# Expert stage of a decoder layer: the fourth and fifth product of each step change places

## The chip, the cores and the metric

One core of a Trainium2 chip runs the whole layer as one program. The metric is the device time of the program in microseconds, the median of several runs. TensorE is called PE here, VectorE DVE, ScalarE ACT, GpSimd POOL, and SyncE SP; SP issues the loads of the weights. All engines run on their own and meet in semaphores.

## What is computed

A decoder layer on 512 tokens of width 1024: attention and a state-space branch, merged and projected back, then a mixture of 32 experts of which each token takes four. Only the expert stage matters here. The reference gathers the rows of each expert and does, for each of them:

```python
gu = xb @ w1[e] + b1[e]                      # 1024 -> 2048
gate, up = gu[:, :D_EXPERT], gu[:, D_EXPERT:]
gate = jnp.minimum(gate, SWIGLU_LIMIT)
up = jnp.clip(up, -SWIGLU_LIMIT, SWIGLU_LIMIT)
act = (up + 1.0) * (gate * jax.nn.sigmoid(SWIGLU_ALPHA * gate))
yb = act @ w2[e] + b2[e]                     # 1024 -> 1024
return yb * wts[:, None].astype(yb.dtype)
```

All weights are float32: w1 of one expert is 8 MiB, w2 is 4 MiB, so the 32 experts have 384 MiB.

## The kernel before

The expert stage is the last block of the kernel. The experts are ranked by the number of their rows and taken in pairs, one from the 16 with most rows ("big", room for 112 rows) and one from the rest ("small", room for 64). Weights come in units of 1 MiB, twelve for an expert: eight of w1 (`(1, n)`, 128 rows of 8 KB) and four of w2 (`(2, n)`, 256 rows of 4 KB).

A big expert's unit is split before it is used: ACT copies the raw unit to a rounded high part (`split_at`, line 1970), DVE makes the low part as raw less high (line 2087), and PE multiplies three times, high by high, low by high and high by low (line 1854 for w1, 1866 for w2). The raw slot is free once DVE is done. A small expert's unit is multiplied in float32 as it is (line 1874 for w1, 1883 for w2), two column groups of PE side by side; its slot is free when PE is done.

The stage runs in steps of twelve units, an S step and a B step in turn, 15 pairs of steps in a loop and a last S step behind it. An S step does w1 of the small expert and w2 of the big one before it; a B step does w1 of the next big expert and w2 of the small one. Which unit stands at which of a step's twelve positions is written out by hand in `STEP` (line 45): an entry `(1, n)` is a unit of the expert whose w1 is due, `(2, n)` one of the expert whose w2 is due. So in an S step the entries `(1, n)` are small and the entries `(2, n)` big, in a B step the reverse. `PLACE` (line 47) turns a position into the running number of that expert's kind.

Four engines walk through the same list:

- SP (`step`, line 1744) issues the load of each position into one of six raw slots in turn (`RAW`, `slot_of`). It first waits in `freed` for the unit six positions earlier: for DVE's low part if that was a big expert's unit, for PE's product if it was a small one's. Loads are issued at line 1728.
- ACT and DVE (`step_s`, `step_b`) take the big expert's units of the step in order, into three split buffers (`SPLIT`). ACT's high part waits for the load, and for PE to have used the unit three before.
- PE (`unit`, `step_s`, `step_b`) takes all twelve. Ahead of the first entry `(2, n)` (`FIRST2`) it writes the bias of the second product into its bank: `bias2_b` in an S step (line 1840), `bias2_s` in a B step (line 1846). Behind the last `(1, n)` (`LAST1`) it transposes the next rows.

POOL gathers the rows of the next experts by indirect DMA, and makes the tiles that pick an expert's bias (`pick_big`, `pick_small`), each after a wait for a count of units used. Results go out by DMAs that ACT issues (lines 2017 and 2026). ACT has the evacuations of the banks in the same list as its splits, at places that don't depend on `STEP` beyond their being ahead of or behind its units.

Of the kernel before, what the change touches and what calls it, by code (L numbers as in the profile page):

```python
# [41 lines left out]
NB = E + NOV + 1  # L42
YROWS = NBIG * CAP + NSM * CS
FILL = NOV * CAP // 7
STEP = ((1, 0), (1, 1), (1, 2), (2, 0), (1, 3), (1, 4), (1, 5), (2, 1), (1, 6), (1, 7), (2, 2), (2, 3))
FIRST2, LAST1 = STEP.index((2, 0)), STEP.index((1, 7))
PLACE = {"S": [("S", n) if m == 1 else ("B", n) for m, n in STEP],
         "B": [("B", 4 + n) if m == 1 else ("S", KT + n) for m, n in STEP]}
RAW, SPLIT = 6, 3
# [112 lines left out]
def decoder_layer(nc, x, small, consts, onehot_rows, gffn, rel_bias, par, w_mix, w_dt, w_tail, w_rt, w1, w2, b12,  # L162
                  tok_ids, pads, out):
    with ExitStack() as ctx:
# [1513 lines left out]
        with nc.Block() as block:  # L1678
# [37 lines left out]
            def _(sp):  # L1716
# [13 lines left out]
                def freed(j, kind, p):  # L1730

                    q = p + (12 if kind == "B" else 0) - RAW
                    if q < 0 and isinstance(j, int) and j == 0:
                        sp.wait_ge(lo_ready, KT + q + 1)
                        return
                    if q < 0:
                        j, q = j - 1, q + 24
                    of, i = PLACE["S" if q < 12 else "B"][q % 12]
                    if of == "B":
                        sp.wait_ge(lo_ready, b_unit(j, i) + 1)  # L1740
                    else:
                        sp.wait_ge(s_used, s_unit(j, i) + 1)

                def step(j, kind, e1, e2):
                    for p, (m, n) in enumerate(STEP):
                        freed(j, kind, p)
                        load(slot_of(kind, p), m, n, e1 if m == 1 else e2)
# [33 lines left out]
            def _(pe):  # L1781
# [106 lines left out]
                def unit(j, kind, p):  # L1888

                    m, n = STEP[p]  # L1890
                    of, i = PLACE[kind][p]
# [72 lines left out]
            def _(act):  # L1964
# [7 lines left out]
                def split(j, kind, p):  # L1972

                    of, i = PLACE[kind][p]
                    assert of == "B"
                    split_at(b_unit(j, i), (KT + i) % SPLIT, slot_of(kind, p), landed(j, kind, p))
# [52 lines left out]
                def step_s(j, more):  # L2029
# [3 lines left out]
                    for p in range(12):  # L2033
                        if STEP[p][0] == 2:
                            split(j, "S", p)
# [333 lines left out]
```

## Time and profile before

| | us |
|---|---|
| three runs | 2086.09, 2095.89, 2097.14 |
| median | 2095.89 |
| profiled execution, its span | 2092.0 |
| expert stage in it, about | 980 to 2052 |

The page gives the span of the profiled execution from its first to its last instruction; a time with what lies around the span isn't shown for it. In the page's 40 slices a slice is 52.3 us, and a digit is the busy share in tenths. PE is busy 90% of the span, DVE 52%, ACT 45%, POOL 13%. The mean granted clock of TensorE is 0.955 of 2.4 GHz. "Releaser" is what ended an engine's idle time; a load's time to landing runs from its issue by SP to its last byte, and so holds the time that it queues behind other loads.

### The profile page before, as it was taken

How to read it: one execution, taken by the hardware profiler on the slowest of the kernel's cores; microseconds unless marked ns; L12 is line 12 of the kernel's file. 1: busy time of each engine (PE TensorE's matmuls, PEld its weight loads, DVE VectorE, ACT ScalarE, POOL GpSimd, SP SyncE). 2: the span in 40 equal slices, each digit the busy share in tenths (PEclk: the TensorE clock that was granted, in tenths of full speed). 3: DMA queues.
4: the chain of work that ended last, by engine and by line, in shares of the span. 5: the costliest groups of instructions: out<-in, count | busy, mean ns of one | idle time of the engine just before them, and what ended most of it. 6: DMA issues, size and time to landing. Idle time of an engine off the chain costs nothing.

```text
span 2092.0 us, 27150 instructions
## 1 busy us (share of the span) xinstructions
PE 1875.1 (90%) x8654; PEld 1313.1 (63%) x8654; DVE 1097.2 (52%) x1343; ACT 949.8 (45%) x1350; POOL 276.5 (13%) x327
## 2 busy tenths in 40 slices
PE   7999999999989999871999999999999998999991
PEld 5887887788767888661656555565555655565550
DVE  6557756855755333325545544554435544455443
ACT  5566666666655222311535443454434443354430
POOL 0312222231220000004000000011001110011002
PEclk9999999999999999975999999999999999999996
DMA  5023122212203222431899999999999999999996
GB/s 200 31 88 118 40 96 100 90 54 91 88 10 101 100 90 100 153 157 52 336 404 397 408 394 403 393 407 397 398 406 395 409 394 405 398 396 404 407 397 227
DMA packets 110267, 519.66 MB, mean 248 GB/s; under 512 B 14912, under 2 KB 18024, under 8 KB 77240
## 3 DMA queue, kind: packets, MB, share of 16 engines
q1 hardware_dynamic: 99480, 487.76, 60.0%
q0 software_dynamic: 6144, 19.94, 3.1%
q10 hardware_dynamic: 4608, 11.54, 1.4%
q8 instruction: 17, 0.28, 0.1%
q14 instruction: 18, 0.15, 0.0%
HBM read 502.98 MB, written 26.49 MB: 253 GB/s over the span
## 4 chain that ended last, share of the span: by engine, by line
DMA 20%; PE 19%; DVE 6%; ACT 4%; issue 3%; POOL 1%; ACTq 0%; SPq 0%; POOLq 0%; DVEq 0%
DMA big<-in_w 19%; PE bank L1854 9%; DVE w_lo L2087 5%; PE bank L1866 4%; PE bank L1874 4%; ACT w_hi L1970 3%; PE bank L1883 2%; POOL big L2261 1%; DVE x_lo L2099 1%; DMA big<-y_all,last_idx 0%; DVE keep L2124 0%; ACT keep L1997 0%; DVE keep L2184 0%; PE bank L1809 0%; PE bank L1790 0%
## 5 line engine op out<-in xcount | busy, mean ns | idle before, releaser
L2087 DVE TENSOR_TENSOR w_lo<-big,w_hi 128x2048 fp32r<-128x2048 f32 x192 | 439.0, 2294 | 417.7 <-ACT w_hi L1970 417.4
L1970 ACT ACTIVATE w_hi<-big 128x2048 fp32r<-128x2048 f32 x192 | 366.3, 1916 | 431.4 <-DMA big<-in_w 405.5
L1874 PE MATMUL bank<-big,keep 128*64 128x512 f32 x1024 | 230.9, 598 | 0.0
L1117 PE MATMUL bank<-h_hi,wm_hi 128*128 128x512 f32 x384 | 157.2, 409 | 4.1 <-DVE wend L898 2.9
L1874 PEld LDWEIGHTS bank<-big,keep 128*64 128x64 f32 x1024 | 69.3, 137 | 137.8 <-issue 137.8
L1854 PE MATMUL bank<-w_hi,x_hi 128*128 128x512 f32 x512 | 146.9, 409 | 8.9 <-DVE w_lo L2087 8.5
L1117 PE MATMUL bank<-h_hi,wm_lo 128*128 128x512 f32 x384 | 151.0, 393 | 0.0
L1117 PE MATMUL bank<-h_lo,wm_hi 128*128 128x512 f32 x384 | 150.3, 391 | 0.0
L1866 PE MATMUL bank<-w_hi,a_hi 128*128 128x512 f32 x256 | 91.4, 440 | 59.2 <-DVE w_lo L2087 58.9
L1854 PE MATMUL bank<-w_lo,x_hi 128*128 128x512 f32 x512 | 138.6, 393 | 0.0
L1854 PE MATMUL bank<-w_hi,x_lo 128*128 128x512 f32 x512 | 137.9, 391 | 0.0
L1854 PEld LDWEIGHTS bank<-w_hi,x_hi 128*128 128x128 f32 x512 | 91.2, 189 | 64.4 <-DVE w_lo L2087 43.1
L1883 PE MATMUL bank<-big,keep 128*64 128x512 f32 x512 | 120.0, 602 | 0.0
L1499 DVE TENSOR_TENSOR g_lo<-keep,g_hi 128x1024 fp32r<-128x1024 f32 x39 | 47.8, 1225 | 125.2 <-ACT g_hi L1424 122.8
L1854 PEld LDWEIGHTS bank<-w_lo,x_hi 128*128 128x128 f32 x512 | 96.7, 189 | 21.6
L1854 PEld LDWEIGHTS bank<-w_hi,x_lo 128*128 128x128 f32 x512 | 96.7, 189 | 20.9
L1866 PEld LDWEIGHTS bank<-w_hi,a_hi 128*128 128x128 f32 x256 | 48.1, 204 | 89.8 <-DVE w_lo L2087 81.9
L837 DVE SCALAR_TENSOR_TENSOR big<-bank,par_sb,big 128x511 f32<-128x511 f32 (+2 forms) x96 | 71.7, 747 | 31.7 <-ACT big L588 23.2
L1117 PEld LDWEIGHTS bank<-h_hi,wm_hi 128*128 128x128 f32 x384 | 72.5, 189 | 24.5 <-issue 5.8
L1144 PE MATMUL bank<-vz_hi,h_hi 128*128 128x384 f32 x256 | 87.2, 341 | 0.0
L1866 PE MATMUL bank<-w_lo,a_hi 128*128 128x512 f32 x256 | 85.9, 419 | 0.0
L1144 PE MATMUL bank<-vz_hi,h_lo 128*128 128x384 f32 x256 | 85.9, 336 | 0.0
(314 smaller groups left out, 3306.9 us busy)
## 6 DMA issues: line engine op xcount, KB each, us to landing
big<-in_w SPq DMA_DIRECT2D x384, 1024.0 KB, 10.5
big<-in_w_mix SPq DMA_DIRECT2D x72, 512.0 KB, 3.3
keep<-in_w_tail SPq DMA_DIRECT2D x47, 512.0 KB, 3.2
y_all<-in_x SPq DMA_DIRECT2D x7, 1280.0 KB, 7.9
y_all<-keep ACTq DMA_DIRECT2D x16, 448.0 KB, 8.1
y_all<-keep ACTq DMA_DIRECT2D x32, 128.0 KB, 7.1
keep<-in_x SPq DMA_DIRECT2D x4, 512.0 KB, 4.9
big<-in_x SPq DMA_DIRECT2D x4, 512.0 KB, 4.5
```

The costliest lines, as they stand in the source:

```text
L837: ins = dve.scalar_tensor_tensor(out=conv[:, n, s:T], in0=proj_b[n % 2][:, 0:T - s], scalar=w, in1=conv[:, n, s:T], op0=ALU.mult, op1=ALU.add)
L1117: ins = pe.matmul(proj_b[n % 2][:], w[:, k], h[:, k], start=(k == 0 and w is hi and h is h_hi), stop=(k == KT - 1 and w is lo))
L1144: ins = pe.matmul(proj_b[t % 2][:, 0:VZ], h[:, k, t * P:(t + 1) * P], w[:, k], start=(k == 0 and h is h_hi and w is hi), stop=(k == KT - 1 ...
L1499: dve.tensor_tensor(lo, graw[:, m % GRAW], hi.bitcast(F32), ALU.subtract).then_inc(glo_ready.sem, 1)
L1854: ins = pe.matmul(bank[c][:], x_part, w_part[:, s, c * 512:(c + 1) * 512], start=False, stop=n == KT - 1 and w_part is w_hi and x_part is lo)
L1866: ins = pe.matmul(bank[4 + c][:], a_part, w_part[:, s, o:o + 512], start=False, stop=k == KT - 1 and w_part is w_hi and a_part is lo)
L1874: ins = pe.matmul(bank[2 * (c // 2)][r, :], x_s[:, n], raw[:, s, c * 512:(c + 1) * 512], start=False, stop=n == KT - 1)
L1883: ins = pe.matmul(bank[4][CS * c:CS * (c + 1), :], a_s[:, k % 4, CS * (k // 4):CS * (k // 4 + 1)], raw[:, s, o:o + 512], start=False, stop ...
L1970: act.activation(w_hi[:, s], raw[:, r], ACT.Copy).then_inc(hi_ready, 1)
L2087: dve.tensor_tensor(w_lo[:, s], raw[:, r], w_hi[:, s].bitcast(F32), ALU.subtract).then_inc(lo_ready, 1)
L2099: dve.tensor_tensor(lo[:, k, 0:CAP], turned(half), hi[:, k, 0:CAP].bitcast(F32), ALU.subtract).then_inc(done.sem, 1)
L2261: pool.indirect_dma_start(fin[:, n], None, y_all, bass.IndirectOffsetOnAxis(ap=last_idx[:, n:n + 1], axis=0)).then_inc(fin_in[n // TOPK], 16)
```

## The change

In `STEP` the entries `(2, 0)` and `(1, 3)` at positions 3 and 4 (counted from 0) change places. `FIRST2` is computed from the list and goes from 3 to 4; `LAST1` stays 9. Everything that walks through `STEP` or `PLACE` follows: loads and their slots, splits, products. In an S step the four products at the start are then small, small, small, small, and the big expert's first w2 unit is fifth; in a B step four big ones stand at the start, and the small expert's first w2 unit is fifth. No instruction is added or removed.

```diff
-STEP = ((1, 0), (1, 1), (1, 2), (2, 0), (1, 3), (1, 4), (1, 5), (2, 1), (1, 6), (1, 7), (2, 2), (2, 3))
+STEP = ((1, 0), (1, 1), (1, 2), (1, 3), (2, 0), (1, 4), (1, 5), (2, 1), (1, 6), (1, 7), (2, 2), (2, 3))
 FIRST2, LAST1 = STEP.index((2, 0)), STEP.index((1, 7))
 PLACE = {"S": [("S", n) if m == 1 else ("B", n) for m, n in STEP],
          "B": [("B", 4 + n) if m == 1 else ("S", KT + n) for m, n in STEP]}
```

## Rows read from the trace of the kernel before

**Rows 1.** The page: span, and busy tenths of PE and DMA by slice.

```profile
span 2092.0 us, 27150 instructions
...
PE   7999999999989999871999999999999998999991
...
DMA  5023122212203222431899999999999999999996
```

**Rows 2.** Windows of two pairs of steps, with the columns.

```profile
core 0: us, PE busy (x) PEld busy (x) DVE busy (x) ACT busy (x) POOL busy (x), PEclk, DMA share, GB/s
1203.60:1270.30 66.70, 61.76 (x283) 36.96 (x282) 33.42 (x22) 28.74 (x24) 5.50 (x8) 1.00 1.02 399
...
1403.70:1470.20 66.50, 62.45 (x279) 37.43 (x278) 33.33 (x22) 28.73 (x24) 7.75 (x8) 0.97 1.02 401
```

**Rows 3.** DMA view, 1203.6 to 1270.3: rate in 40 slices, packets, loads' queue.

```profile
GB/s 432 423 423 398 381 236 243 383 410 426 434 393 423 440 408 418 398 413 420 430 437 393 432 398 425 322 302 283 420 437 440 386 427 435 403 423 400 415 408 437
DMA packets 4975, 26.60 MB, mean 399 GB/s; under 512 B 464, under 2 KB 464, under 8 KB 2928
...
q1 hardware_dynamic: 4479, 25.16, 95.2%
```

**Rows 4.** Loads (line 1728) to landing: 1060 to 1980; the one at 1018.8.

```profile
DMA to landing us min/median/max: 5.8/10.6/14.0
...
DMA to landing us min/median/max: 4.8/4.8/4.8
```

**Rows 5.** Chain of waits, last S step: start, duration, what.

```profile
2013.39 9.32 DMA big<-in_w
...
2024.68 2.30 DVE w_lo L2087
...
2035.24 5.69 PE bank L1866 x24
```

**Rows 6.** Timeline, S step: start, duration, engine, line; idle before in brackets.

```profile
1416.34 1.91 ACT L1970 ACTIVATE w_hi<-big 128x2048 fp32r<-128x2048 f32 x1 [3.87 <-DMA big<-in_w]
...
1417.07 0.50 PE L1840 MATMUL bank<-bias_hl,pick_b 64*128 64x512 f32 x2
1418.28 2.29 DVE L2087 TENSOR_TENSOR w_lo<-big,w_hi 128x2048 fp32r<-128x2048 f32 x1 [5.54 <-ACT w_hi L1970]
...
1420.63 1.22 PE L1866 MATMUL bank<-w_hi,a_hi 128*128 128x512 f32 x2 [3.06 <-DVE w_lo L2087]
...
1431.03 0.74 PE L1866 MATMUL bank<-w_hi,a_hi 128*128 128x512 f32 x2 [0.62 <-DVE w_lo L2087]
```

**Rows 7.** Window of the w2 unit at position 3, columns as in rows 2.

```profile
1420.60:1425.00 4.40, 4.37 (x12) 3.28 (x12) 0.00 (x0) 0.00 (x0) 0.00 (x0) 0.64 1.01 414
```

**Rows 8.** Loads: S position 4; S 9 to 11; B position 3, issued 1437.8.

```profile
L1728 SPq DMA_DIRECT2D big<-in_w x1: 333/333/333, 1408.9 to 1408.9; - x1
...
DMA to landing us min/median/max: 9.9/9.9/9.9
...
L1728 SPq DMA_DIRECT2D big<-in_w x3: 333/384/384, 1420.7 to 1428.9; - x3
...
DMA to landing us min/median/max: 7.0/7.8/10.9
...
DMA to landing us min/median/max: 10.0/10.0/10.0
```

**Rows 9.** Timeline, start of the B step.

```profile
1448.90 2.29 DVE L2087 TENSOR_TENSOR w_lo<-big,w_hi 128x2048 fp32r<-128x2048 f32 x1 [1.07 <-ACT w_hi L1970]
...
1451.70 1.92 ACT L1970 ACTIVATE w_hi<-big 128x2048 fp32r<-128x2048 f32 x1 [2.83 <-DMA big<-in_w]
...
1454.08 0.39 PE L1846 MATMUL bank<-bias_hl,pick_s 128*128 128x512 f32 x1
1454.39 1.94 PE L1883 MATMUL bank<-big,keep 128*64 128x512 f32 x8
...
1457.05 2.29 DVE L2087 TENSOR_TENSOR w_lo<-big,w_hi 128x2048 fp32r<-128x2048 f32 x1 [1.11 <-ACT w_hi L1970]
```

## The prediction

> **What bounds the kernel now.** Read the page first: the last 19 of its 40 slices, the expert stage, show PE and DMA both at 9 tenths or more [rows 1]. The change lives there only, so the question is which of the two sets its pace. The windows over pairs of experts answer it: of four pairs in a row the first takes 66.7 us and the last 66.5, the DMA share is 1.02 in both, 399 and 401 GB/s are moved, and PE is busy for 61.8 and 62.5 us [rows 2]. PE has some 4 us to spare in each pair; the DMA engines have none. The DMA view of one pair says what fills them: of 26.60 MB the 24 weight loads of 1 MiB are 25.16, and gathered rows and results written out the other 1.44 [rows 3]. Where neither crosses, the slices of that view lie around 420 GB/s, so a load needs 1.049 MB / 420 GB/s = 2.5 us; 24 of them are 60 us, and the other 6.6 us are what 1.44 MB in short pieces cost.
>
> Being busy isn't enough: a queue that runs dry now and then would show as well. So look at how far ahead the loads are issued. From 1060 to 1980 us a load lands 5.8 to 14.0 us after its issue, median 10.6 [rows 4]. A load that found the queue empty (1018.8 us, after the gap at the start of the stage) landed in 4.8 us [rows 4]. The smallest distance of 920 us, 5.8, is 1.0 us above that, so before every load another one was still under way. The queue never runs dry. That SP waits between its loads, with six slots taken, is then the sign of a full queue and not of a late release.
>
> The chain of waits names ACT, DVE and PE behind a load, since it runs from the load through the split to the product and back to the slot [rows 5]. That a slot's release stands on it doesn't make the release late: the load that it permits has 7 us and more of other loads ahead of it.
>
> **The change, part by part.** In an S step the first unit of the big expert's w2 (call it B0; w2 of the big expert, split into a high and a low part) goes from position 3 to 4, and the small expert's w1 unit n=3 (S3) from 4 to 3. In a B step the same swap puts the big expert's w1 unit 3 ahead of the small expert's first w2 unit. Instructions, bytes, slots and split buffers are the same in number: 0 us of work are added or removed. The order is read by SP (loads), ACT and DVE (splits) and PE (products), so all four move together; POOL's list doesn't move, but two of its waits count units (lines 2223 and 2229, the tiles that pick the bias) and end one unit, up to 3 us, later. Both tiles are next read by a bias product at the start of a later step, with seven units between, so at 2.5 us and more a unit they still come over 14 us early; without that cover PE would wait those 3 us.
>
> *S step, by the pair at 1404 us.* PE waits 3.06 us for B0's low part [rows 6]: the load of position 3 landed at 1416.3, where ACT's idle ends; ACT's high part took 1.91, DVE's low part 2.29, PE began at 1420.63. Its three S units had ended by 1417.07, the bias product by 1417.57. An S unit takes PE 1.8: the three between B0's end at 1425.0 [rows 7] and the idle before B1 take 1431.03 - 0.62 - 1425.0 = 5.4 us. After the change the load of position 3 holds S3, needs no split, and PE multiplies it at once: 1417.1 + 1.8 = 1418.9; bias 0.5, to 1419.4. B0 is now the load of position 4, which lands at 1408.9 + 9.9 = 1418.8 [rows 8]; through ACT and DVE (1.91 + 2.29 and some 0.08 between) it is ready at 1423.1. So the wait before B0 does not go: it is 1423.1 - 1419.4 = 3.7 us, 0.6 longer, as the load moves back by one place (2.5 us) and one S unit takes only 1.8. B0 then takes 4.4 us as before [rows 7] (to 1427.5), S4 and S5 take 3.6 (to 1431.1). B1 is a position that doesn't move: PE began it at 1431.03, after 0.62 us of idle that DVE's low part ended. After: 1431.1. The longer wait before B0 is taken from the idle before B1, and behind B1 nothing is changed. Sum for PE: 0.1 us late at most, and the queue has 7 us in hand for that.
>
> *Its slots.* Six slots in turn, so position 9 waits for position 3, 10 for 4, 11 for 5, and the next step's 0 for 6. Position 9: before when B0's low part was made (issue 1420.7), after when S3 is used (1418.9). Position 10: before when S3 was used (1425.0 + 1.8, so issued at 1427, to landing 7.0 us, the shortest of this pair), after when B0 is split (1423.1): 4 us earlier. Position 11: before 1428.9 with 7.8 us to landing, after S4's use at 1429.3: 0.5 us later, 7.3 [rows 8]. So the shortest distance goes from 7.0 to 7.3, against 4.8 for a queue just empty. The margin is a little wider, and a wider margin on a full queue is worth 0 us.
>
> *B step.* PE does w1 units 0 to 2, then from 1454.08 the bias (0.4 us), the S unit, and unit 3 behind it [rows 9]. After, unit 3 is the load of position 3, which landed at 1437.8 + 10.0 = 1447.8 [rows 8]; DVE is free of unit 2 at 1448.90 + 2.29 = 1451.2, so unit 3's low part is ready at about 1453.5, and PE begins it without idle at 1454.0, where the bias stood. A B unit takes 2.85 (5.69 for two [rows 5]): to 1456.8; bias 0.4 and S unit 1.8 to 1459.0, with the S unit's load (position 4) landed when ACT's idle ends, at 1451.7 [rows 9]. Unit 4's low part is ready at 1457.05 + 2.29 = 1459.34 in both orders, and PE can't begin unit 4 before. Again 0. Position 10 is now freed by the S unit, at 1459.0, position 9 by a split, at 1453.5; position 10's load would be issued some 2 us later than now, with those of positions 8 and 9 still queued in front of it. 0 us.
>
> *Start and end.* The stage's only dry spot is at its start: the load at 1018.8 waits for the first S unit's use. Positions 0 to 2 are untouched, so it stays where it is; position 9 would wait for one S unit more, about 1 us, with two loads ahead of it. 0 us. The end hangs on B1 of the last S step (load issued at 2013.39, landed 9.32 later, DVE's part at 2024.68), then on two S units, B2, B3, the results and four S units [rows 5]; all stand at unmoved positions. 0 us.
>
> *What no row shows.* Which load is under way while results and gathered rows cross the engines. In the S step these 0.52 MB (64 rows of 4 KB gathered, as much written) press the rate to 236 and 243 GB/s for two slices of 1.67 us, in the B step 0.92 MB (112 rows each way) press it to 322, 302, 283 for three [rows 3]. Against 420 that is 2 x 1.67 x 180/420 = 1.4 us and 3 x 1.67 x 118/420 = 1.4 us. In the S step w1 rows of 8 KB take the place of w2 rows of 4 KB in that spot. Bounds: a gain of the whole 1.4 us a pair, or nothing; as a loss, the same 1.4 once more. The value taken is 0, since in the B step positions 4 and 5 are w1 loads already and the dip is there all the same.
>
> The Trainium skill speaks to this ("DMA: Bandwidth & Descriptors", Queues, rings and completion order): each DMA engine takes turns between its queues, a whole packet at a time. By that rule larger pieces in the load's queue would win it a larger share while a write is pending and only delay the write, for which nobody waits; the engines' total stays and the sum stays 0. No row here separates share from total.
>
> **The rivals.** *Faster:* the S step's dip goes, as the load that meets the writes has larger pieces. For it: per byte the S dip costs nearly twice the B dip. Against it: the B dip stands with w1 loads. At the full price 15 pairs x 1.4 = 21 us, 2075; if it only falls to the B step's cost per byte, 0.6 x 15 = 9 us, 2087.
>
> *Slower:* TensorE's clock. After the waits before B0 the granted clock is low: it is 0.64 of 2.4 GHz from 1420.6 to 1425.0, that is mostly the 1.2 GHz level, and B0's 12 products take 4.4 us [rows 7] where B units run at 2.85 [rows 5]. The pair at 1203 us had 1.00 in the mean and PE busy 61.8, those after 0.97 [rows 2], so not each wait brings it. A wait of 3.7 us could bring it each time and keep it through S4 and S5: 3.6 us more for the two, and for B0 0.6 to 1.5 more where it now runs at full clock in part or whole. PE's 62.5 would become 66.1 to 67.6 in a pair of 66.5: PE would take over as the bound with up to 1.1 us a pair, 16 us over 15 pairs: 2112. It decides where PE's busy time of a pair passes 66.5. Against it: once PE is late, it waits less before B0, and the clock stays up.
>
> The Trainium skill warns of the same ("TensorE: Matmul & The Clock Gate", Part 1: The HAM clock gate): the slow clock is the default and activity releases it. That the low level follows the idle wait here agrees with it; by that page alone a longer wait would speak for this rival, at the price above.
>
> *It doesn't do what it says:* the swap would fill PE's wait before B0 with S3 if the loads stayed where they are, 1.8 us of 3.06. They move with it, and PE isn't the bound: even with them left in place no time would be won.
>
> **How the numbers follow.** The profiled span is 2092.0 us; the runs' median is 2095.9, 0.2% above, and the runs reach from 2086.1 to 2097.1. Change 0 + 0 + 0 = 0: 2092.0 for a profiled execution, 2095.9 for the median. Forecast (DMA remains the bound, nothing shifts): 0.76, by itself 2087 to 2103. Faster rival: 0.12. Slower rival: 0.12. The range for 8 in 10 takes in the nearer part of both: 2080 to 2106. A measurement of this kernel can tell some 0.5% (10 us) from no change; beyond that: faster 0.12, within 0.76, slower 0.12.
>
> **What would show it.** In the profile after: pairs of 66.5 us and a DMA share of 1.02; the wait before B0 still there, at 3.3 to 4.0 us; idle before B1 gone; the shortest time from issue to landing above 5 us; PE's busy time of a pair below 64. The forecast is wrong if a pair takes 65.1 (the dip gone) or over 67.5 with PE busy throughout, or if loads land in under 5 us.

## The result, and the profile after

The changed kernel took 2084.23 us in the median (2080.85 to 2086.80), the kernel before 2094.97 beside it: a ratio of 0.995, interval 0.9926 to 0.9974. Timed again beside each other, with more runs, the same two kernels stood at 2085.00 and 2090.82, ratio 0.997, interval 0.9955 to 0.9986. The change is a small gain of 0.3 to 0.5%, some 6 to 11 us. The forecast was no change (2095.9). Its range of 2080 to 2106 held the time, but only because it took in part of a rival; that there would be no change was wrong.

The page of the kernel after, where it answers to [rows 1]:

```profile
span 2080.8 us, 27121 instructions
...
PE   7999999999988999870999999999999999999991
...
DMA  6023122212202322531899999999999999999995
```

Nothing moved there: PE and DMA are both full through the expert stage. Of the 11.2 us between the spans 2.1 lie ahead of the stage (its seventh load is issued at 988.7 before and 986.5 after), which the change doesn't touch. The rest lies in the pairs. Two pairs after, columns as in [rows 2]:

```profile
1202.00:1267.60 65.60, 61.91 (x273) 36.86 (x272) 33.23 (x22) 28.88 (x24) 6.71 (x8) 0.95 1.01 398
...
1398.90:1465.30 66.40, 62.52 (x276) 37.63 (x275) 33.24 (x22) 28.89 (x24) 6.57 (x8) 0.95 1.01 399
```

The engines' work is the same, the DMA share is full, and still a pair is done sooner: the DMA engines need less time for the same bytes. The landings of the loads tell where. From the issue and the time to landing of each load (as in [rows 4, 8]) the interval between any two landings follows; the means over 14 pairs, in us:

| stretch | before | after |
|---|---|---|
| S step, positions 3 to 6 (four loads) | 12.85 | 12.50 |
| B step, positions 3 to 6 | 13.22 | 12.88 |
| the other 16 loads of the pair | 40.24 | 40.28 |
| pair | 66.3 | 65.7 |

One profile a kernel is thin evidence for such a table: a second profile of the unchanged kernel, taken later, has 12.38, 13.12, 40.23 and 65.7 us in these four rows. So the pair's 0.6 us isn't told from scatter, and neither is the S row; only the B row, checked over more profiles below, holds.

Four loads alone on the engines take 4 x 2.49 = 10.0 us. In both stretches something else crosses: a gather of token rows, and then the results. The DMA view of 1060 to 1980 us has the time to landing of both gathers, first before, then after (`s_idx` is the small expert's gather, `g_idx` the big one's; the last number is the median from issue to landing):

```profile
keep<-h_rows,s_idx POOLq DMA_INDIRECT x14, 8.2
keep<-h_rows,g_idx POOLq DMA_INDIRECT x13, 9.5
```

```profile
keep<-h_rows,s_idx POOLq DMA_INDIRECT x14, 7.7
keep<-h_rows,g_idx POOLq DMA_INDIRECT x13, 8.0
```

The big gather landed 1.5 us sooner. The rate in 40 slices of 0.6 us, about one big gather, before (1436 to 1460 us) and after (1431 to 1455):

```profile
GB/s 430 396 410 423 423 423 423 423 423 423 369 416 416 410 423 430 437 287 294 294 314 328 321 355 314 451 444 403 437 451 437 423 369 396 410 430 430 416 430 423
```

```profile
GB/s 300 410 396 423 423 423 410 423 423 437 423 437 423 437 437 423 403 266 314 294 294 348 348 444 451 355 478 410 416 410 451 437 437 416 376 403 403 444 451 389
```

The dip is as deep as before (266 to 348 GB/s against 287 to 355) but six slices long in place of eight (with a single slice of 355 two slices behind). While the gather is on, the engines move some 300 GB/s, not 420; what makes its crossing shorter saves time for the whole stream. So the question for the experiments was: what shortens it?

The trace also counts the packets (one for each row that is moved). Here is the DMA view of one big gather from its first row to its last, 1511.5 to 1516.1 before, then 1507.1 to 1510.3 after; q0 is the gathers' queue:

```profile
DMA packets 274, 1.50 MB, mean 325 GB/s; under 512 B 30, under 2 KB 30, under 8 KB 153
...
q0 software_dynamic: 126, 0.46, 31.3%
```

```profile
DMA packets 275, 1.04 MB, mean 326 GB/s; under 512 B 23, under 2 KB 23, under 8 KB 272
...
q0 software_dynamic: 127, 0.46, 44.8%
```

The packets under 2 KB carry next to nothing. In both views 112 of those between 2 and 8 KB are the gathered rows. What is left are the loads' rows: 121 of 8 KB and 11 of 4 KB before, 3 of 8 KB and 137 of 4 KB after. So beside each gathered row about one row of the loads passes, be it long or short, at the same total rate; with short ones the same gather is through in 3.1 us and not in 4.4. The loads' rows that pass are those of position 4 (w1 before, w2 after), though position 3 lands only 2.6 us after the gather's first row (1514.2 against 1511.6) in this pair before: a load's rows cross well ahead of its landing.

The results have no part in the dip. Their rows (q10) cross behind it, in the B step of the pair at 1203 us before from 1250.3 to 1255:

```profile
DMA packets 340, 2.02 MB, mean 431 GB/s; under 512 B 37, under 2 KB 37, under 8 KB 149
...
q10 hardware_dynamic: 128, 0.46, 23.9%
```

The other steps of the forecast, in the timeline of the pair at 1399 us:

```profile
1418.34 1.22 PE L1866 MATMUL bank<-w_hi,a_hi 128*128 128x512 f32 x2 [3.70 <-DVE w_lo L2087]
...
1423.76 3.73 PE L1874 MATMUL bank<-big,keep 128*64 128x512 f32 x16
...
1427.42 0.73 PE L1866 MATMUL bank<-w_hi,a_hi 128*128 128x512 f32 x2
```

PE waits 3.70 us before B0, and no longer before B1, as forecast; B0 takes 5.4 us (1418.34 to 1423.76), 1 us more than before. PE's busy time of a pair hardly moved: 62.5 and 61.9 us in the windows above, 62.5 and 61.8 before [rows 2].

### The profile page after: what moved, and what is told of

It reads as the page before. It is cut to its first block, busy times and chain, and to the rows that moved or that the text cites. A ratio compares the mean times of both kernels' runs of the same rounds, so it can differ in the third digit from the quotient of the medians.

```text
span 2080.8 us, 27121 instructions
## 1 busy us (share of the span) xinstructions
PE 1873.9 (90%) x8654; PEld 1315.7 (63%) x8654; DVE 1095.8 (53%) x1343; ACT 949.4 (46%) x1350; POOL 279.3 (13%) x327
## 4 chain that ended last, share of the span: by engine, by line
PE 27%; DMA 15%; DVE 5%; ACT 3%; issue 2%; POOL 1%; ACTq 0%; SPq 0%; POOLq 0%; DVEq 0%
DMA big<-in_w 14%; PE bank L1854 14%; PE bank L1866 5%; PE bank L1883 4%; DVE w_lo L2087 4%; PE bank L1874 3%; ACT w_hi L1970 3%; POOL big L2261 1%; PE bank L1797 0%; DMA big<-y_all,last_idx 0%; DVE x_lo L2099 0%; DVE keep L2184 0%; DVE keep L2124 0%; PE bank L1790 0%; ACT keep L2014 0%
## 5 line engine op out<-in xcount | busy, mean ns | idle before, releaser
L1866 PE MATMUL bank<-w_hi,a_lo 128*128 128x512 f32 x256 | 87.3, 425 | 0.0
```

The costliest lines, as they stand in the source:

```text
L1866: ins = pe.matmul(bank[4 + c][:], a_part, w_part[:, s, o:o + 512], start=False, stop=k == KT - 1 and w_part is w_hi and a_part is lo)
```

## The experiments

Each was timed beside the kernel before on its chip, and the ratio is to that kernel. How finely a ratio can be read, the unchanged kernel tells: timed in the same way against itself it stood at 1.0011 (0.9997 to 1.0024). "B stretch" is the time of the four loads at B positions 3 to 6, "S stretch" the same in the S step, both as above.

### Loads or products

First theory (A): the DMA engines are the bound, and a gather costs less against w1's rows of 8 KB, which now stand at position 3, than against w2's of 4 KB. Rival (B): PE's new order frees a slot earlier. The load order and the product order can be changed apart:

```diff
+PROD = <the other order>
-FIRST2, LAST1 = STEP.index((2, 0)), STEP.index((1, 7))
+FIRST2, LAST1 = PROD.index((2, 0)), PROD.index((1, 7))
...
-                    m, n = STEP[p]
+                    m, n = PROD[p]
+                    p = STEP.index((m, n))
```

> Loads in the new order, products in the old one (slots, splits and waits follow the loads). Theory A (the DMA engines stay the bound, and a gather of token rows costs them less while loads with rows of 8 KB are in the queue than with rows of 4 KB): the whole gain of the change, ratio to the kernel before 0.994 to 0.997; a gathered row set lands as fast as in the changed kernel. Rival B (the gain comes from PE's order: it frees a slot earlier): no gain, 0.999 to 1.002. Rival C (nothing but scatter between runs): 1.000.

Measured: 2122.03 us, ratio 1.0152 (1.0131 to 1.0173).

> Loads in the old order, products in the new one. Theory A: no gain, 0.999 to 1.002, gathers as slow as in the kernel before. Rival B: 0.994 to 0.997. Rival C: 1.000.

Measured: 2106.36 us, ratio 1.0077 (1.0059 to 1.0094).

Both were slower, which neither theory had. From 1060 to 1980 us the loads' time to landing was, in the first and in the second:

```profile
DMA to landing us min/median/max: 4.7/10.6/14.1
...
DMA to landing us min/median/max: 4.7/9.7/14.3
```

4.7 us is the time of a load that finds nothing, or as good as nothing, ahead of it [rows 4]. With the loads new and the products old, S position 9 waits for the slot of the w1 unit that is loaded first but multiplied only behind B0: in the pair at 1404 us it is issued at 1439.54, after the load before it had landed (1438.96), and the landing behind it comes 5.3 us later in place of 2.5. The other way round it is B position 9 (issued 1465.28, the load before it lands at 1466.58). Once a pair the queue ran dry, and a pair took 68.3 and 67.0 us (before 66.3): this is what it costs when the loads aren't issued far enough ahead. The runs don't tell A from B by time. But the B stretch fell to 12.93 us with the new load order and was 13.27 with the old: the gain goes with the order of the loads. The time to landing says the opposite, 10.4 us for the big gather with the new load order (9.4 with the old). In the packets its rows cross in 3.6 us (4.2 with the old order), but the first of them 6.1 us after the gather's issue, where it is 4.1 to 4.2 us in all other runs; why it starts late there isn't shown. So it is the crossing that counts, and the time to landing stands for it only where the start is the same.

### The length of the rows

> The kernel before with w2 laid out so that its loads have rows of 8 KB as those of w1; order, bytes and waits unchanged. Theory A: gathers get as short as in the changed kernel or shorter, which is worth 0.6 us a pair or 10 us, and the 8 w2 loads of a pair take 2.49 in place of 2.55 us, worth 0.5 us a pair or 7 us: together some 2078, ratio 0.990 to 0.994. Rivals B and C: only the second part, 0.996 to 0.998.

```diff
-                        src = w2[bass.ds(e, 1), 2 * n:2 * n + 2].rearrange("a k p n -> p (a k) n")
-                        dst = raw[:, s].rearrange("p (k n) -> p k n", k=2)
+                        src = w2[bass.ds(e, 1), n].rearrange("a p n -> (a p) n")
+                        dst = raw[:, s]
...
-    w2 = np.asarray(i["w2"][0]).reshape(E, 8, P, D)
+    w2 = np.asarray(i["w2"][0]).reshape(E, 4, 2, P, D).transpose(0, 1, 3, 2, 4).reshape(E, 4, P, 2 * D)
```

Measured: 2087.00 us, ratio 0.9974 (0.9962 to 0.9986), as rivals B and C had it. The gathers landed in 8.2 and 9.3 us, as before: only the second part came, that w2's loads get as fast as w1's (2.49 in place of 2.55 us). Theory A falls: rows of 8 KB at position 3 don't make a gather cheap.

> The changed kernel with the same w2 layout. Theory A: the order no longer matters, so the same time as the kernel before with that layout (within 0.2%), ratio 0.990 to 0.994. Rival B: the two gains add, 0.4 to 0.5% below the kernel before with that layout.

Measured: 2083.36 us, ratio 0.9959 (0.9943 to 0.9975). The big gather took 9.3 us here too. This is the changed kernel's order, and its gain at the big gather is gone: it hung on w2 having rows of 4 KB. The time is above the expected 0.990 to 0.994, since no gather got cheaper, and not told from the run before it. So a new theory (D): a gather is cheap where *short* rows are queued, and the change put them right: position 4, not 3.

> The changed kernel with w1 laid out so that all its loads have rows of 4 KB like those of w2. Theory D (a gather shares the engines with the loads for a shorter time where the loads in the queue have short rows; the changed kernel has a w2 load at position 4, right where the big gather runs, and that is why its big gather lands in 8.0 in place of 9.5 us): both gathers land as fast or faster than in the changed kernel (big 8.0 us or less, small 7.5 or less). The 16 w1 loads of a pair take 2.55 in place of 2.49 us, 1.0 us a pair, so 0.998 to 1.003 of the kernel before. Rival E (row length has no part in it, only the instant at which a gather is issued): gathers as in the changed kernel or in the one before (9.5 us), 1.002 to 1.007.

```diff
-    w1 = np.asarray(i["w1"][0]).reshape(E, KT, P, 2 * D)
+    w1 = np.asarray(i["w1"][0]).reshape(E, KT, P, 2, D).transpose(0, 1, 3, 2, 4)
```

(and the load as w2's.) Measured: 2094.98 us, ratio 1.0018 (1.0005 to 1.0032); gathers 7.4 and 7.8 us, loads 2.56 us each. As theory D has it, on both counts. By itself the run doesn't exclude rival E, which allowed the changed kernel's gathers and a time from 1.002 on.

### One step at a time, and the change once more

> The swap in S steps alone. Theory D with the small gather's part: the four loads at S positions 3 to 6 take 12.5 in place of 12.85 us, B steps as in the kernel before (13.2): half of the gain, ratio 0.997 to 0.999. If the two steps are coupled by the queue, the queue runs dry in places as it did with loads and products in different orders: slower than the kernel before.

Measured: 2088.68 us, ratio 0.9991 (0.9978 to 1.0004).

> The swap in B steps alone. Theory D: the four loads at B positions 3 to 6 take 12.9 in place of 13.2 us and the big gather lands in about 8.0 us, S steps as before: the other half, ratio 0.997 to 0.999. If the steps are coupled: slower than the kernel before.

Measured: 2087.87 us, ratio 0.9977 (0.9963 to 0.9992).

The edit of both is one table for each kind of step in place of `STEP`:

```diff
+ORD = {"S": <one order>, "B": <the other>}
...
-                    for p, (m, n) in enumerate(STEP):
+                    for p, (m, n) in enumerate(ORD[kind]):
...
-                    m, n = STEP[p]
+                    m, n = ORD[kind][p]
```

The big gather in the traces, first with the swap in S steps, then in B steps:

```profile
keep<-h_rows,g_idx POOLq DMA_INDIRECT x13, 9.4
```

```profile
keep<-h_rows,g_idx POOLq DMA_INDIRECT x13, 8.0
```

The big gather follows the B step alone (B stretch 13.20 and 12.80 us). The steps aren't coupled. The S swap by itself isn't told from no change.

> The changed kernel itself once more, beside the kernel before on the same chip. If the gain is one of the order, 0.994 to 0.998; if it was scatter between runs, 0.999 to 1.001.

Measured: 2085.00 us, ratio 0.997 (0.9955 to 0.9986), big gather 7.9 us, B stretch 12.82. Clear of no change, and about the sum of the two parts (0.09 and 0.23%).

### Which load's rows

Theory F: what counts is the row length at position 4, whatever unit stands there. In the old order, w1's unit 3 alone is laid out in rows of 4 KB:

```diff
+    w1[:, 3] = w1[:, 3].reshape(E, P, 2, D).transpose(0, 2, 1, 3).reshape(E, P, 2 * D)
...
+                        if n == 3:
+                            src = w1[bass.ds(e, 1), n].rearrange("a p n -> a (p n)").rearrange(
+                                "a (k p n) -> p (a k) n", k=2, p=P)
```

> The kernel before, old order, with w1's unit 3 alone (the load at position 4 of both steps) laid out in rows of 4 KB. Theory F (a gather is cheap where the load at position 4 has rows of 4 KB, whatever unit that is; runs so far: rows of 4 KB there 7.9 to 8.0 us to landing for the big gather, rows of 8 KB 9.3 to 9.5): big gather 7.8 to 8.1 us, small one 7.4 to 7.7, a pair 0.6 to 0.8 us shorter for the gathers and 0.1 longer for the rows: 0.996 to 0.998. Rival G (the order itself, by what PE frees when): gathers 9.4 and 8.2 us as in the kernel before, 1.000 to 1.001.

Measured: 2089.80 us, ratio 0.9983 (0.9967 to 1.0). The big gather, and the packets of one of them from its first row to its last (1443.3 to 1446.2), then the same for the kernel before with w2 in rows of 8 KB (1440.4 to 1444.5):

```profile
keep<-h_rows,g_idx POOLq DMA_INDIRECT x13, 8.0
...
DMA packets 252, 0.99 MB, mean 342 GB/s; under 512 B 10, under 2 KB 10, under 8 KB 252
```

```profile
DMA packets 245, 1.38 MB, mean 336 GB/s; under 512 B 21, under 2 KB 21, under 8 KB 133
```

The big gather is as fast as in the changed kernel, and the B stretch 12.88 us, with no product and no load moved. Its rows start at the same instant as in the kernel before, 1.3 us behind the landing of position 2 (medians of 13 gathers), so rival E, that the instant of a gather decides, falls, and with the order unchanged rival G too. No row of 8 KB passes beside the gather now, and all 112 rows are through in 2.9 us. In the old order with long rows everywhere 112 rows of 8 KB pass with it, which takes 4.0 us. The small gather took 7.8 us, longer than the expected 7.4 to 7.7. The time agrees in sign, but its interval reaches no change.

> The kernel before, old order, with w1's unit 4 (position 5) in rows of 4 KB, position 4 as it was (8 KB). Theory F (position 4 alone decides, as the gather's rows are taken in turn with the load behind the one that is landing): big gather 9.3 to 9.5 us, 1.000 to 1.001. If any short rows in the stretch help: big gather 8.0 to 8.6 us, 0.997 to 0.999.

(The same edit with unit 4.) Measured: 2093.82 us, ratio 1.002 (1.0008 to 1.0031), big gather 9.2 us, B stretch 13.19. The time is a little above the expected 1.000 to 1.001, and next to the unchanged kernel's 1.0011 of the same set; two loads a pair that take 0.06 us longer are an estimated 0.1% more. Short rows at position 5 bring nothing, and at position 3 the kernel before had them already. Position 4 decides.

> The changed kernel with w2's units 1 to 3 in rows of 8 KB and unit 0 (position 4) left in rows of 4 KB. Theory F: gathers as in the changed kernel (big 7.9 us) and six loads a pair at 2.49 in place of 2.55 us, 0.36 us a pair, 5 us: 0.994 to 0.995 of the kernel before, faster than both kernels. Rival G: the same, so this run is for a better kernel, and tells F only from a theory in which all four w2 units matter (then big gather 9.3 us and 0.996).

(w2's layout of the first row-length run for units 1 to 3, unit 0 as it was, in the changed order.) Measured: 2080.91 us, ratio 0.9956 (0.9941 to 0.9972), big gather 7.8 us. The fastest median of all runs, by a hair: it isn't told from the changed kernel by its interval. It also isn't told by time from the run with w2 in long rows throughout (0.9959), though its big gather is 1.5 us and its B stretch 0.2 us shorter; 0.2 us in 15 pairs are 3 us or 0.15%, which both intervals leave room for.

### The small gather

> The kernel before with five short operations of POOL (about 1 us) ahead of each small gather. Theory H (for the small gather the instant counts too: its first row crossed the engines 0.2 us after a landing in the kernel before and about 1 us after one in the changed kernel, where it is cheap): the four loads at S positions 3 to 6 take 12.3 to 12.5 in place of 12.85 us, 0.997 to 0.999. If the load that it meets alone decides: 12.85 us as before, 1.000.

The added operations (their tile `spare` is made wider for them):

```diff
+                    if n == 1:
+                        for k in range(3, 8):
+                            pool.tensor_tensor(spare[:, k:k + 1], spare[:, 2:3], spare[:, 2:3], ALU.add)
```

Measured: 2090.41 us, ratio 0.9998 (0.9986 to 1.001); S stretch 12.37 us. The stretch fell as theory H had it, the time did not.

> The kernel before, unchanged, as a yardstick: ratio 0.999 to 1.001 against itself; big gather 9.3 to 9.5 us to landing, small 8.1 to 8.3; four loads at S positions 3 to 6 in 12.7 to 12.9 us, at B positions 3 to 6 in 13.1 to 13.3. If these scatter by 0.3 us, the small gather's part of the gain isn't told from scatter.

Measured: 2092.15 us, ratio 1.0011 (0.9997 to 1.0024) of the same kernel. Its gathers and stretches: small 7.8 us and 12.38, big 9.4 and 13.12. The small gather's two were expected at 8.1 to 8.3 and 12.7 to 12.9.

The S stretch of one and the same kernel scatters from 12.85 to 12.38 us between two profiles. So the S part of the table at the top (12.85 to 12.50) is not shown to come from the change, and neither is that of the late gather. The B part stands apart from scatter. All profiles, by what stands at position 4 of the B step; the crossing is the time from the gather's first row to its last, the median of 13 gathers:

| at position 4 | big gather lands, us | its rows cross in, us | B stretch, us | runs |
|---|---|---|---|---|
| rows of 8 KB, w2 elsewhere 4 KB | 9.2 to 9.5 | 4.2 to 4.4 | 13.12 to 13.27 | before, before again, products new, swap in S, late gather, unit 4 short |
| rows of 8 KB everywhere | 9.3 | 4.2 to 4.4 | 13.02, 13.03 | w2 long, in both orders |
| rows of 4 KB | 7.8 to 8.0 | 2.9 to 3.2 | 12.80 to 12.95 | after, again, swap in B, unit 3 short, w2 long but unit 0, w1 short |
| rows of 4 KB, queue dry once a pair | 10.4 | 3.6 | 12.93 | loads new, products old |

In all 15 profiles 111 to 138 of the loads' rows (medians) pass while the 112 gathered rows cross, and the rate is 312 to 334 GB/s meanwhile. Against 421 GB/s for loads alone (1.049 MB in 2.49 us) a crossing that is 1.2 us shorter at 320 GB/s saves an estimated 1.2 x (1 - 320/421) = 0.3 us, most of the 0.35 by which the B stretch fell.

## Why the prediction was wrong

*The bound* was right: DMA share full, PE with 4 us to spare, the other 16 loads of a pair unmoved at 40.2 us.

*PE, slots, start and end* were right in kind. The wait before B0 is 3.70 us for a forecast 3.7, it goes on in all pairs (16 waits of line 1866, 47.4 us, from 1060 to 1980), and the wait before B1 is gone. Mis-sized was position 11's distance: 7.3 us forecast, measured

```profile
L1728 SPq DMA_DIRECT2D big<-in_w x1: 384/384/384, 1426.0 to 1426.0; - x1
...
DMA to landing us min/median/max: 5.8/5.8/5.8
```

since B0 took 5.4 us in place of 4.4 and S4 was used 1 us late. This pair is at the low end: the mean over 14 pairs is 7.0 us. The window of that unit, columns as in [rows 2], where [rows 7] had a clock of 0.64:

```profile
1418.30:1423.70 5.40, 5.36 (x12) 3.84 (x12) 0.00 (x0) 1.84 (x1) 0.00 (x0) 0.50 1.03 420
```

The whole unit ran at the 1.2 GHz level. The clock's mean over a pair went from 0.97 to 0.95, so the slower rival's mechanism did act, for about 1 us of the 4 that it would have needed to make PE the bound, and the full queue hid it, with 1 us left (5.8 us to landing against 4.8 for an empty queue).

*"What no row shows" is the step that failed.* It priced the one thing that the change does to the DMA engines, which load is under way while a gather crosses, at 0. Its reason was that the B step's dip stands although w1 loads are at positions 4 and 5. That row was read the wrong way about: the dip was long *because* a w1 load was at position 4, and the change puts w2 there. The forecast looked at the load that lands during the gather (position 3) and at longer rows, where the runs show the load behind it and shorter rows. The bound given, up to 1.4 us a pair, held the size: 0.35 us a B step (13.2 to 12.85 over the profiles), 5 us in 15 pairs, 0.25% of the kernel, as the swap in B steps alone gave (0.23%). The dips were also laid to the wrong traffic, "112 rows each way": the results cross behind them, at 431 GB/s, and a dip is the gather alone.

The rule of turns between queues was used there to argue that the engines' total stays, so that only the shares move. The total did not stay: eight slices of some 300 GB/s became six. A share matters when the other party, the gather, runs the engines below their rate as long as it lasts. That about one row of the loads passes for each gathered row, whatever its length, fits the rule in the Trainium skill ("DMA: Bandwidth & Descriptors", Queues, rings and completion order) that an engine changes queues only at packet boundaries; the trace shows the ratio over the whole gather, 112 rows to 111 to 138, and not one engine's order. The forecast had asked whom longer rows delay and took it to be a write that costs nothing; it is the gather, and it costs rate as long as it lasts. Why position 4 decides and not 3 is in the packets too: while the big gather crosses, hardly a row of position 3 is left, 11 of its 256 in the gather shown, though it hasn't landed.

*The rivals.* The faster one had the right resource, loads against crossing rows, and a price of 9 to 21 us against 6 to 11 measured. Its cause was wrong: it had the S step, the writes and longer rows, where the part that is shown is in the B step, at the gather, and from shorter rows. Its chance of 0.12 was too low: it was the only part with a resource at its limit and no row for its cost.

*Open.* What makes the small gather's stretch go from 12.85 to 12.4 us within and between runs of one kernel. It falls in the course of the run in several profiles, and the small gather's rows cross in 3.9 us in the one profile and 2.9 in the other (medians); what makes them differ the run with the late gather didn't settle. The S step's part of the gain, 0.09% with an interval that reaches no change, is not shown.

## What to carry to other kernels

When the DMA engines are the bound, an order of loads isn't free of cost because its bytes are the same: look for the stretches with a lower rate (here at the gathers), and count whose packets cross there: here the load behind the one that lands next, and its row length set how long the gather held the rate down. Moving loads and products apart, with slots in turn, emptied the queue once a pair in both tries here; moved together they didn't. Before a gain of a few tenths of a per cent is read from one profile, a second profile of the unchanged kernel is worth its time. And where a change touches a resource at its limit and no row prices that, a zero isn't the careful choice.

## What the runs showed of the hardware

- A gather of 112 rows of 4 KB beside a stream of loads landed 7.8 to 8.0 us after its issue where the load one behind the landing one had rows of 4 KB, and 9.2 to 9.5 us where it had rows of 8 KB (14 of 15 profiles; the one in which the queue ran dry stands apart). Its rows crossed in 2.9 to 3.2 us and in 4.2 to 4.4 us, with 111 to 138 rows of the loads beside the 112, and the engines moved 312 to 334 GB/s in place of 421 meanwhile. With the short rows the stream lost some 0.35 us less.
- Results of 0.46 MB, written beside the loads, didn't lower the rate: 431 GB/s while they crossed, in the one stretch looked at.
- The same 1 MiB took 2.49 us in rows of 8 KB and 2.55 to 2.56 in rows of 4 KB.
- In the changed kernel, with 5.6 us or more from each load's issue to its landing, the stream hid 3.7 us of idle a pair and a slower clock on PE. With 4.7 us once a pair the kernels were 0.8 and 1.5% slower.
